# Expert outputs of a decoder trunk on one Trainium2 core: rows scattered to token order from GpSimd's queue, or whole slot blocks stored from ScalarE's queue and gathered by token at the end

## The chip, the cores and the metric

One Trainium2 chip, one core. The time is device microseconds of one launch, from run to run; the kernel before took 1139.21 us (median of 3 runs, 1138.52 to 1142.39).

## What is computed

A decoder layer on 512 tokens of width 1024 in float32: a mixed attention and recurrent stage, a cross-attention into 256 memory tokens, and a mixture of experts, each followed by a layer norm of `ALPHA*x + result`. Only the last stage is touched. Its reference, cut:

```
e_idx, gate = route(xf, w_router, b_router)      # best of 8 groups, then top-2 of its 4 experts
# for each expert e, over the rows (tokens) that chose it:
h = jax.nn.silu(xb @ w_gate[e]) * (xb @ w_up[e])
y = h @ w_down[e]
# back to tokens, each row weighted by its gate, the two rows of a token added:
y = segment_sum(y * row_gate[:, None], row_tok)
x = layer_norm(ALPHA * x + y, ln_g[l, 2], ln_b[l, 2])
```

There are 32 experts, each with gate and up weights of 1024 x 512 and down weights of 512 x 1024: 6 MB for an expert, 192 MB in all. The 512 tokens choose 2 experts each, so 1024 rows exist, 32 for an expert on average.

## The kernel before, in words

All times and lines here are of the last stage, from about 605 us on.

**Slots.** Each expert gets a block of `CAP` = 64 slots. A table `tabs` (128 x 32 x 4) holds for each slot of each expert the token, the destination row and the two factors (gate, and ALPHA for the first choice of a token). It is made by matmuls of one-hot masks (`token_columns`, L1425; `row_and_gate_columns`, L1432) that DVE reads out of PSUM (L1439, L1443 to L1447). Empty slots get indices beyond the bounds. A token that overflows 64 slots is handled by `further_blocks`, a loop that runs only if some expert has more than 64 rows; in the profiled execution it does not run.

**Weights.** SP alone issues the weights, in pieces of 1 MB (128 partitions x 8 KB), in the order of use (`stream`, `load_piece`, L1482) into 21 places. For piece n it waits until its place is free and until piece n-4 has landed (`piece_here(sp, n - 4)`, L1485), so about four pieces are outstanding.

**One expert.** POOL gathers its token rows with an indirect DMA from DRAM (`xs_rows`) into 64 partitions of `xg` (`rows_in`, L1771). PE turns them (L2003, L2004), ACT copies the result (`tokens`, L2229), PE multiplies gate and up (`gate_up`, L2020), ACT takes the silu (L2234), DVE the product (L2450), PE turns that, DVE copies (L2454), PE multiplies down (`down`, L2030), and DVE scales by the gate and adds ALPHA times the token rows that ACT has prepared (`first_rows`, L2241) into `ye` (`out_rows`, L2464). `ye` is 128 x 512: partitions 0 to 63 hold the first half of the 64 result rows, 64 to 127 the second. It has two buffers.

**Results out.** After each expert POOL waits for DVE and scatters `ye` with an indirect DMA into `y_rows`, a DRAM table in token order (row = choice, token, half; 2 KB each), L1776. Empty slots are skipped. In POOL's program the gather for expert e+2 stands ahead of the scatter of expert e. The last two experts (30 and 31) are different: only their ALPHA part (`xrow`) is scattered, their products are brought into token order by PE (`combined`, L2125).

**The tail.** SP waits for all scatters (`rows_out`, `late_out`), then loads `y_rows` back in four transfers of 1 MB, one for each 128 tokens (`yb[t]`, L1708), with the gain and offset of the layer norm between the second and the third (L1707). DVE or PE add the two rows of each token (L2506, L2118), the layer norm follows (DVE L2513 to L2530, ACT L2299), and SP stores the output (L1711).

## Time and profile before

| what | value |
|---|---|
| median of 3 runs | 1139.21 us (1138.52 to 1142.39) |
| span of the profiled execution | 1135.4 us |
| its own time as a run | not recorded apart; the median is 3.8 us above the span |
| PE busy | 1058.4 us, 93% |
| DVE / ACT / POOL busy | 345.5 / 273.6 / 85.8 us |
| the core's DMA, whole span | 263.31 MB, 232 GB/s |
| HBM read / written | 257.60 / 13.05 MB |

The span runs from the first to the last instruction; a run's time has some microseconds of launch around it. MB are millions of bytes, while a weight piece is 1024 KB. "DMA share" is the mean busy share of the core's 16 DMA engines; it can pass 1 a little where transfers of an engine overlap. "PEclk" is TensorE's granted clock as a share of 2.4 GHz. SPq, ACTq and POOLq are the queues' issuing side. The number in square brackets behind a row of the timeline is the time for which the engine stood idle before it, and who ended that.

### The profile page before, as it was taken

Reading aid. Unit: us, or ns where it says so; the run is one execution under the profiler, and the core shown is the slowest. Engines: PE = TensorE matmul, PEld = TensorE weight load, DVE = VectorE, ACT = ScalarE, POOL = GpSimd, SP = SyncE. Lnnn points to the kernel's source line nnn. Section 1 sums busy time; section 2 is a strip of 40 time slices with the busy share of each in tenths; the row PEclk is TensorE's granted clock in tenths of the full one; section 3 lists DMA queues with packets and bytes.
Section 4 is the critical chain, followed back from the end, with each engine's and each line's share of the span. In section 5 each row is a group of like instructions: output and inputs, shape, how many; then the busy total and the mean of one; then the engine's idle time right before and its main releaser. Section 6 shows DMA issues by size and latency. Waiting matters only on the chain.

```text
span 1135.4 us, 15981 instructions
## 1 busy us (share of the span) xinstructions
PE 1058.4 (93%) x6710; PEld 533.3 (47%) x6710; DVE 345.5 (30%) x729; ACT 273.6 (24%) x540; POOL 85.8 (8%) x133
## 2 busy tenths in 40 slices
PE   9999999999899999999998999999998898898896
PEld 4444455566655544566446544444443333333332
DVE  0179522334664453104146211111111011011116
ACT  2431122234454500023202211222111011011123
POOL 2000100000000000100000211111111101101110
PEclk9999999999999999999999899999999989989999
DMA  8112220222024320923316999999999999999996
GB/s 278 37 41 86 97 76 2 76 76 76 14 64 149 110 77 1 361 84 117 148 74 257 368 398 404 403 394 393 393 396 392 401 395 394 399 396 401 398 401 251
DMA packets 55847, 263.31 MB, mean 232 GB/s; under 512 B 7250, under 2 KB 8402, under 8 KB 30944
## 3 DMA queue, kind: packets, MB, share of 16 engines
q1 hardware_dynamic: 49424, 252.81, 57.8%
q0 software_dynamic: 5120, 8.40, 2.3%
q8 instruction: 54, 0.88, 0.3%
q10 hardware_dynamic: 1232, 1.07, 0.3%
q14 instruction: 17, 0.14, 0.0%
HBM read 257.60 MB, written 13.05 MB: 238 GB/s over the span
## 4 chain that ended last, share of the span: by engine, by line
PE 31%; DMA 24%; DVE 3%; issue 1%; ACT 1%; SPq 0%; POOLq 0%; ACTq 0%; DVEq 0%
DMA ring<-in_w_exp_up 7%; PE cpair L2020 5%; PE bank L2030 5%; PE tpair L2020 4%; DMA ar<-in_w_exp_up 3%; PE bank L1861 2%; PE bank L1841 2%; DMA mixT<-in_w_exp_down 2%; DMA ring<-in_w_exp_down 2%; DMA avq<-in_w_exp_up 2%; PE tpair L1861 1%; PE bank L1834 1%; PE cpair L1861 1%; PE tpair L1841 1%; PE cpair L1841 1%; DMA mixT<-y_rows 1%
## 5 line engine op out<-in xcount | busy, mean ns | idle before, releaser
L2020 PE MATMUL cpair<-ring,xgT 128*64 128x512 f32 x312 | 82.8, 594 | 7.6 <-DMA ring<-in_w_exp_up 4.4
L2234 ACT ACTIVATE hs<-cpair 64x512 f32<-64x512 f32 x21 | 12.4, 589 | 237.7 <-PE cpair L2020 237.7
L2464 DVE SCALAR_TENSOR_TENSOR ye<-bank,tabs,xgt 128x512 f32<-128x512 f32 x30 | 22.5, 751 | 136.0 <-PE bank L2030 136.0
L2030 PE MATMUL bank<-ring,hT 128*64 128x512 f32 x224 | 57.6, 656 | 6.2 <-DVE hT L2454 6.2
L2450 DVE TENSOR_TENSOR hs<-cpair,hs 64x512 f32<-64x512 f32 x21 | 14.6, 693 | 154.3 <-ACT hs L2234 154.3
L922 PE MATMUL bank<-xT,ring 128*128 128x512 f32 x128 | 60.9, 606 | 0.0
L1776 POOL DMA_INDIRECT y_rows<-ye,tabs x30 | 30.3, 1011 | 383.8 <-DVE ye L2464 383.8
L2020 PEld LDWEIGHTS cpair<-ring,xgT 128*64 128x64 f32 x312 | 26.2, 137 | 53.1 <-issue 52.0
L365 PE MATMUL bank<-xT,ring 128*128 128x512 f32 x112 | 48.5, 593 | 0.0
L2241 ACT ACTIVATE xgt<-xgt,tabs 64x512 f32<-64x512 f32 x64 | 46.0, 719 | 1.6
L2020 PE MATMUL tpair<-ring,xgT 128*64 128x512 f32 x152 | 39.5, 594 | 4.5 <-DMA ring<-in_w_exp_up 2.5
L941 PE MATMUL tpair<-ring,mixT 128*128 128x512 f32 x96 | 42.0, 593 | 0.0
L1012 ACT ACTIVATE pcb<-tpair 128x512 f32<-128x512 f32 (+1 forms) x32 | 17.4, 544 | 77.3 <-DVE pcb L1180 77.2
L2450 DVE TENSOR_TENSOR hs<-tpair,hs 64x512 f32<-64x512 f32 x11 | 7.6, 693 | 90.7 <-ACT hs L2234 90.7
L2030 PEld LDWEIGHTS bank<-ring,hT 128*64 128x64 f32 x224 | 16.5, 151 | 37.6 <-issue 29.8
L365 PEld LDWEIGHTS bank<-xT,ring 128*128 128x128 f32 x112 | 21.2, 190 | 27.1 <-issue 26.3
L2229 ACT ACTIVATE xgT<-tpair 128x512 f32<-128x512 f32 x32 | 19.1, 597 | 58.4 <-PE tpair L2004 58.4
L2004 PEld LDWEIGHTS tpair<-ident,xgt 64*128 64x128 f32 x224 | 32.5, 223 | 0.0
L2234 ACT ACTIVATE hs<-tpair 64x512 f32<-64x512 f32 x11 | 6.5, 588 | 107.6 <-PE tpair L2020 107.6
L922 PEld LDWEIGHTS bank<-xT,ring 128*128 128x128 f32 x128 | 22.3, 190 | 20.7 <-issue 19.8
L1771 POOL DMA_INDIRECT xgt<-xs_rows,tabs x31 | 29.6, 955 | 15.7 <-issue 9.0
L911 PE MATMUL bank<-memT,ring 128*128 128x256 f32 x128 | 30.7, 383 | 0.0
(471 smaller groups left out, 1894.7 us busy)
## 6 DMA issues: line engine op xcount, KB each, us to landing
ring<-in_w_exp_gate SPq DMA_DIRECT2D x30, 1024.0 KB, 11.1
ring<-in_w_exp_down SPq DMA_DIRECT2D x30, 1024.0 KB, 11.1
ring<-in_w_exp_up SPq DMA_DIRECT2D x28, 1024.0 KB, 11.2
ring<-in_w_in SPq DMA_DIRECT2D x6, 2048.0 KB, 8.1
ring<-in_w_mem_kv SPq DMA_DIRECT2D x4, 2048.0 KB, 10.3
mixT<-in_w_exp_down SPq DMA_DIRECT2D x7, 1024.0 KB, 10.3
ar<-in_w_exp_down SPq DMA_DIRECT2D x7, 1024.0 KB, 11.0
xT<-in_w_exp_gate SPq DMA_DIRECT2D x6, 1024.0 KB, 11.5
```

The costliest lines, as they stand in the source:

```text
L365: last = nc.tensor.matmul(dst[:, :], w[:, k, j * P:(j + 1) * P], xT[:, k, :], start=(k == 0), stop=(k == KT - 1))
L911: last = nc.tensor.matmul(dst[:, a * MEM:(a + 1) * MEM], slot(GKV + i // 2, 512)[:, k, ct * P:(ct + 1) * P], memT[:, k, :], start=(k == 0) ...
L922: last = nc.tensor.matmul(dst[:, :], lhs, rhs, start=(k == 0), stop=(k == KT - 1))
L941: last = nc.tensor.matmul(wo_bank[i % 3][:, :], mixT[:, k, t * P:(t + 1) * P], slot(GO + hf, 512)[:, k, :], start=(k == 0), stop=(k == 2 * ...
L1771: return pool.indirect_dma_start(dst, None, xs_rows[:, :], bass.IndirectOffsetOnAxis(idx.bitcast(U32), 0), bounds_check=below(S), oob_is_e ...
L1776: return pool.indirect_dma_start(y_rows[:, :], bass.IndirectOffsetOnAxis(idx.bitcast(U32), 0), src, None, bounds_check=below(TOP_K * S * 2 ...
L1841: last = nc.tensor.matmul(bank[NT * hf + t][:, :], omT[:, k, t * P:(t + 1) * P], w[:, k, :], start=(k == 0), stop=(k == KT - 1))
L1861: last = nc.tensor.matmul(bank[i][:, cs], w[:, k, (i % 4) * P:(i % 4 + 1) * P], x1T[:, k, cs], start=(k == 0), stop=(k == KT - 1))
L2004: return nc.tensor.transpose(dst, src, ident[rows, rows])
L2020: last = nc.tensor.matmul(bank[b][m * CAP:(m + 1) * CAP, :], xgT[:, k, :], w(m, h)[:, j * DE:(j + 1) * DE], start=(k == 0), stop=(k == KT ...
L2030: last = nc.tensor.matmul(bank[b][m * CAP:(m + 1) * CAP, :], ht[:, k, :], w(2, h)[:, o:o + 512], start=(k == 0), stop=(k == FT - 1))
L2241: nc.scalar.activation(xrow[half[h], e % 2, :], xg[half[e % 2], h * 512:(h + 1) * 512], ACT.Copy, scale=tabs[half[e % 2], e, 3:4].bitcast( ...
```

## The change

The table in token order is gone. A new DRAM table `y_first` has one row of 4 KB for every slot of every expert (32 x 64 rows), and `y_further` has the slots of further blocks. Four things happen.

- **Stores.** ACT issues, for each of experts 0 to 29, two plain DMAs (`result_out`): partitions 0 to 63 of `ye` to the first half, and 64 to 127 to the second half of 64 consecutive rows. All 64 slots are stored, filled or not. In ACT's program `result_out(e - 1)` stands ahead of `silu(e)`, and waits for DVE's `y_scaled`. `token_rows_out` does the same for experts 30 and 31. POOL's scatters are gone from the loop, only its gathers are left.
- **Collecting.** When all stores have landed, POOL issues eight indirect gathers of 128 rows x 4 KB from `y_first` into `yb[t]`, two for each t, in place of SP's four loads. SP loads only the layer norm's gain and offset, right behind the weights.
- **Routing.** DVE computes where the two rows of each token lie (`slot_at`): six small operations more, and the two that made the destination rows and the ALPHA factors are gone. The table columns for destinations are gone.
- **The path for overflow** clears `y_further` first and collects from it afterwards; it does not run on this input.

```
-            KEPT = 905
+            KEPT = 904
 
             def __init__(self, flat):
                 self.kept = flat[:, 0:self.KEPT]
                 self.sel_rows = flat[:, 0:768].rearrange("p (k t f e) -> p k t f e", k=TOP_K, t=NT, f=3)
-                self.caps, self.place, self.row_off = flat[:, 768:896], flat[:, 896:904], flat[:, 904:905]
+                self.caps, self.place = flat[:, 768:896], flat[:, 896:904]
                 self.hit = flat[:, 1024:2048].rearrange("p (r c) -> p r c", c=2 * CAP)
+                self.erow = flat[:, 1024:1024 + NE]
...
-        tabs = sb("tabs", [P, NE, 4], I32)
+        toks = sb("toks", [P, NE], I32)
+        gates = sb("gates", [P, 2, NE])
...
-        def tokens_read(dve, n):
+        def tokens_read(dve, to, n):
             dve.wait_ge(tab_full, 2 * n - 1)
-            nc.vector.tensor_scalar(tabs[0:CAP, :, 0], bank[6][0:CAP, 0:NE], float(OFF), None, ALU.add).then_inc(tokens_known, 1)
-
-        def rows_and_gates_read(dve, ls, n):
+            nc.vector.tensor_scalar(to[0:CAP, :], bank[6][0:CAP, 0:NE], float(OFF), None, ALU.add).then_inc(tokens_known, 1)
+
+        def gates_read(dve, to, n):
             dve.wait_ge(tab_full, 2 * n)
-            nc.vector.tensor_scalar(tabs[:, :, 1], bank[7][:, 0:NE], ls.row_off[:, 0:1], None, ALU.add)
-
-            nc.vector.tensor_scalar(tabs[:, :, 3].bitcast(F32), bank[7][:, 0:NE], 2.0 * S - 2.0 * OFF, ALPHA, ALU.is_lt,
-                                    ALU.mult)
-            nc.vector.tensor_copy(tabs[:, :, 2].bitcast(F32), bank[7][:, NE:2 * NE]).then_inc(tabs_done, 1)
+            nc.vector.tensor_copy(to[:, :, :].rearrange("p f e -> p (f e)"), bank[7][:, 0:2 * NE]).then_inc(tabs_done, 1)
...
-        y_rows = nc.dram_tensor("y_rows", (TOP_K * S * 2, D // 2), F32, kind="Internal").ap()
+        SLOTS, FURTHER = NE * CAP, (S // CAP - 1) * NE * CAP
+        y_first = nc.dram_tensor("y_first", (SLOTS, D), F32, kind="Internal").ap()
+        y_further = nc.dram_tensor("y_further", (FURTHER, D), F32, kind="Internal").ap()
+        y_half_rows = y_further.rearrange("r (h c) -> (r h) c", h=2)
...
-                    rows_out(sp)
-                    sp.wait_ge(late_out, 32)
                     down_read(sp, LAST - 2)
                     sp.wait_ge(f_end, more * NE + 1)
-                    for t in range(NT):
-                        if t == 2:
-                            for h, src in enumerate((ln_g, ln_b)):
-                                sp.dma_start(ln3[:, h, :], src[0, 2:3, :].to_broadcast([P, D])).then_inc(n3.here, 16)
-                        sp.dma_start(yb[t], y_v[t * P:(t + 1) * P, :, :]).then_inc(y_read[t], 16)
+                    for h, src in enumerate((ln_g, ln_b)):
+                        sp.dma_start(ln3[:, h, :], src[0, 2:3, :].to_broadcast([P, D])).then_inc(n3.here, 16)
                     for t in range(NT):
                         sp.wait_ge(n3.shifted, t + 1)
                         sp.dma_start(out[0, t * P:(t + 1) * P, :], ob[t]).then_inc(out_done, 16)
...
+                    def collect(dst, src, rows, idx):
+                        return pool.indirect_dma_start(dst, None, src,
+                                                       bass.IndirectOffsetOnAxis(idx.bitcast(U32), 0),
+                                                       bounds_check=below(rows), oob_is_err=False)
...
                         rows_in(e + 2)
-                        pool.wait_ge(y_scaled, e + 1)
-                        scatter(tabs[:, e, 1:2], ye[:, e % 2, :]).then_inc(y_out[e % 2], 16)
...
-                    further_blocks(pool, before, body)
-                    for e in PE_LAST:
-                        pool.wait_ge(x_done, 2 * (e + 1))
-                        scatter(tabs[:, e, 1:2], xrow[:, e % 2, :]).then_inc(late_out, 16)
+                    def after():
+                        for t in range(NT):
+                            for k in range(TOP_K):
+                                r = k * NT + t
+                                collect(yb[t][:, k, :], y_further[:, :], FURTHER, further_at[:, r:r + 1])\
+                                    .then_inc(f_back, 16)
+                        pool.wait_ge(f_back, 16 * TOP_K * NT)
+
+                    further_blocks(pool, before, body, after)
+                    rows_out(pool)
+                    pool.wait_ge(late_out, 64)
+                    down_read(pool, LAST - 2)
+                    for t in range(NT):
+                        for k in range(TOP_K):
+                            r = k * NT + t
+                            collect(yb[t][:, k, :], y_first[:, :], SLOTS, slot_at[:, r:r + 1]).then_inc(y_read[t], 16)
...
                         if t == 2:
-                            pe.wait_ge(y_read[t], 16)
+                            pe.wait_ge(y_read[t], 32)
...
+                    def result_out(e):
+
+                        act.wait_ge(y_scaled, e + 1)
+                        for h in range(2):
+                            act.dma_start(y_first[e * CAP:(e + 1) * CAP, h * 512:(h + 1) * 512], ye[half[h], e % 2, :])\
+                                .then_inc(y_out[e % 2], 16)
+
+                    def token_rows_out(e):
+
+                        act.wait_ge(x_done, 2 * (e + 1))
+                        for h in range(2):
+                            act.dma_start(y_first[e * CAP:(e + 1) * CAP, h * 512:(h + 1) * 512], xrow[half[h], e % 2, :])\
+                                .then_inc(late_out, 16)
...
                     for e in range(LAST - 1):
+                        if e:
+                            result_out(e - 1)
                         silu(e)
...
                             tokens(e + 1)
                             first_rows(e + 1)
+                    result_out(LAST - 2)
...
                     tokens(e)
                     first_rows(e)
+                    token_rows_out(e)
                     gu_read(act, e)
                     tokens(f)
                     first_rows(f)
+                    token_rows_out(f)
...
+                    link(dve, V.tensor_tensor(ohr[:, :, :, :], oh[:, 0:TOP_K, :, :],
+                                              ls.erow[:, :].unsqueeze(1).unsqueeze(1).to_broadcast(wide), ALU.mult))
+                    link(dve, V.tensor_reduce(slot_f[:, :], ohr[:, :, :, :].rearrange("p k t e -> p (k t) e"), AX_X,
+                                              ALU.add))
...
+                    rows = TOP_K * NT
+                    link(dve, V.tensor_tensor(past[:, :, :], ls.thresholds[:, :].unsqueeze(1).to_broadcast([P, rows, S // CAP - 1]),
+                                              ls.place[:, :].unsqueeze(2).to_broadcast([P, rows, S // CAP - 1]), ALU.is_le))
+                    link(dve, V.tensor_tensor(slot_f[:, :], slot_f[:, :], ls.place[:, :], ALU.add))
+                    tokens_read(dve, toks, 1)
+                    link(dve, V.tensor_reduce(blk_of[:, :], past[:, :, :], AX_X, ALU.add))
+                    link(dve, V.scalar_tensor_tensor(slot_at[:, :], blk_of[:, :], float(NE * CAP - CAP), slot_f[:, :], ALU.mult,
+                                                     ALU.add))
...
-                            dve.wait_ge(y_out[e % 2], 16 * (e // 2))
+                            dve.wait_ge(y_out[e % 2], 32 * (e // 2))
```

ACT's queue in the loop over the experts, before: from the silu of one expert to that of the next (`xgt` holds the gathered rows and, in its second half, their scaled copy; `ye` is the result).

```order
L2234 ACTIVATE hs<-cpair 64x512 [waits w_read]
L2229 ACTIVATE xgT<-tpair 128x512 [waits xgt_full]
L2241 ACTIVATE xgt<-xgt,tabs 64x512 [waits y_scaled]
L2241 ACTIVATE xgt<-xgt,tabs 64x512
L2234 ACTIVATE hs<-cpair 64x512 [waits w_read]
L1612 TENSOR_LOAD more_i
```

The same place in the change.

```order
L2267 ACTIVATE hs<-cpair 64x512 [waits w_read]
L2262 ACTIVATE xgT<-tpair 128x512 [waits xgt_full]
L2274 ACTIVATE xgt<-xgt,gates 64x512 [waits y_scaled]
L2274 ACTIVATE xgt<-xgt,gates 64x512
L2281 DMA y_first<-ye 64x512 [waits y_scaled]
L2281 DMA y_first<-ye 64x512
L2267 ACTIVATE hs<-cpair 64x512 [waits w_read]
L2281 DMA y_first<-ye 64x512 [waits y_scaled]
L2281 DMA y_first<-ye 64x512
```

Two DMA issues, the first of them behind a wait for DVE's result, have come in between the scaled rows and the next silu.

POOL's queue at the end of the loop and behind it, before (the overflow branch between them is left out).

```order
L1767 REGISTER_ALU [waits x_done,xgt_full]
L1771 DMA xgt<-xs_rows,tabs 64x1024
L1767 REGISTER_ALU [waits y_scaled]
L1776 DMA y_rows<-ye,tabs 2048x512
L1612 TENSOR_LOAD more_i
...
L1767 REGISTER_ALU [waits x_done]
L1776 DMA y_rows<-xgt,tabs 2048x512
L1767 REGISTER_ALU [waits x_done]
L1776 DMA y_rows<-xgt,tabs 2048x512
L1622 UNCONDITIONAL_BRANCH
```

POOL in the change.

```order
L1775 REGISTER_ALU [waits x_done,xgt_full]
L1779 DMA xgt<-xs_rows,toks 64x1024
L1775 REGISTER_ALU [waits x_done,xgt_full]
L1779 DMA xgt<-xs_rows,toks 64x1024
L1618 TENSOR_LOAD more_i
...
L1775 REGISTER_ALU [waits late_out,w_read,y_out1,y_out0]
L1788 DMA xT<-y_first,blkones 128x1024
L1775 REGISTER_ALU
L1788 DMA xT<-y_first,blkones 128x1024
...
L1775 REGISTER_ALU
L1788 DMA mixT<-y_first,blkones 128x1024
L1630 UNCONDITIONAL_BRANCH
```

The scatters are gone, and eight gathers from `y_first` stand at the end, behind the wait that SP had.

SP's queue behind the last weights, before.

```order
L1703 ISA [waits late_out,w_read,y_out1,y_out0]
L1708 DMA xT<-y_rows 128x2x1024 [waits f_end]
L1708 DMA xT<-y_rows 128x2x1024
L1707 DMA avq<-in_ln_g 128x1024
L1707 DMA avq<-in_ln_b 128x1024
L1708 DMA mixT<-y_rows 128x2x1024 x2
L1711 DMA out<-ring 128x1024 [waits ln2_shifted] x4
L1622 UNCONDITIONAL_BRANCH [waits out_done]
```

SP in the change.

```order
L1714 ISA [waits w_read]
L1716 DMA avq<-in_ln_g 128x1024 [waits f_end]
L1716 DMA avq<-in_ln_b 128x1024
L1719 DMA out<-ring 128x1024 [waits ln2_shifted] x4
L1630 UNCONDITIONAL_BRANCH [waits out_done]
```

The four loads of `y_rows` have left SP, and the gain and offset no longer wait for the scatters.

## Rows read from the trace of the kernel before

**Rows 1.** Stages: window, its length, busy us of each engine, PEclk, DMA share, GB/s

```profile
700.00:800.00 100.00, 96.09 (x462) 40.61 (x460) 13.83 (x22) 18.37 (x28) 14.76 (x15) 1.00 1.02 400
1000.00:1085.00 85.00, 72.48 (x312) 29.49 (x309) 9.72 (x16) 11.08 (x17) 9.82 (x10) 0.93 1.01 402
```

**Rows 2.** Chain that ended last, from 770 us: start us, us, what

```profile
770.17 6.87 PE cpair L2020 x32
783.64 6.87 PE cpair L2020 x32
...
803.81 11.19 DMA ar<-in_w_exp_up
...
1062.53 9.87 DMA ar<-in_w_exp_up
```

**Rows 3.** Waits of SP's queue, 600 to 1136 us: total us, times, longest

```profile
SPq L1485 <- DMA ring<-in_w_exp_down: 63.2, 24, 3.7
```

**Rows 4.** Page, section 3: DMA queues, packets, MB, share of 16 engines

```profile
q1 hardware_dynamic: 49424, 252.81, 57.8%
q0 software_dynamic: 5120, 8.40, 2.3%
```

**Rows 5.** Windows around one scatter and one gather (columns as in 1)

```profile
867.00:870.00 3.00, 2.99 (x14) 1.24 (x16) 0.00 (x0) 0.00 (x0) 1.96 (x2) 1.00 1.02 412
871.50:873.00 1.50, 1.01 (x6) 0.53 (x8) 0.00 (x0) 0.00 (x0) 0.00 (x0) 1.00 1.01 418
873.00:876.00 3.00, 3.00 (x16) 1.16 (x13) 0.00 (x0) 0.33 (x1) 0.00 (x0) 1.00 1.06 303
```

**Rows 6.** Timeline of POOL, the issues of these two, and a gather alone

```profile
635.58 0.93 POOL L1771 DMA_INDIRECT xgt<-xs_rows,tabs  x1 [6.69 <-ACT xgt L2241]
...
867.60 1.01 POOL L1776 DMA_INDIRECT y_rows<-ye,tabs  x1 [11.20 <-DVE ye L2464]
868.91 0.95 POOL L1771 DMA_INDIRECT xgt<-xs_rows,tabs  x1 [0.30 <-issue]
```

**Rows 7.** Windows with a gather alone, and with scatters alone

```profile
635.00:640.00 5.00, 5.00 (x26) 1.58 (x22) 0.00 (x0) 1.06 (x1) 0.93 (x1) 1.00 0.99 328
1090.00:1095.00 5.00, 5.00 (x27) 2.31 (x23) 0.00 (x0) 0.00 (x0) 0.00 (x0) 1.00 1.01 414
```

**Rows 8.** Timeline, the way into the last experts and their scatter

```profile
1084.62 0.75 DVE L2464 SCALAR_TENSOR_TENSOR ye<-bank,tabs,xgt 128x512 f32<-128x512 f32 x1 [5.55 <-PE bank L2030]
1085.95 0.60 ACT L2229 ACTIVATE xgT<-tpair 128x512 f32<-128x512 f32 x1 [9.14 <-PE tpair L2004]
1091.58 8.22 SPq L1482 DMA_DIRECT2D ring<-in_w_exp_down  x4
1097.15 0.57 ACT L2234 ACTIVATE hs<-tpair 64x512 f32<-64x512 f32 x1
1098.02 0.99 POOL L1776 DMA_INDIRECT y_rows<-xgt,tabs  x1 [8.16 <-ACT xgt L2241]
```

**Rows 9.** Timeline, the tail: loads of y_rows and who waited

```profile
1104.64 1.77 SPq L1708 DMA_DIRECT2D xT<-y_rows  x2
1107.46 1.16 SPq L1708 DMA_DIRECT2D mixT<-y_rows  x2
1112.40 1.22 DVE L2506 TENSOR_TENSOR xT<-xT 128x1024 f32<-128x1024 f32 x1 [3.56 <-DMA xT<-y_rows]
1120.60 1.98 PE L2118 MATMUL cpair<-mixT,ident 128*128 128x512 f32 x4 [0.99 <-DMA mixT<-y_rows]
```

**Rows 10.** Timeline, routing

```profile
620.32 0.42 DVE L2403 TENSOR_TENSOR pmT<-oh,bank 128x256 f32<-128x256 f32 x1 [0.84 <-PE bank L1987]
```

**Rows 11.** Window in the tail (columns as in 1)

```profile
1115.00:1120.00 5.00, 4.61 (x22) 1.74 (x18) 4.45 (x8) 1.54 (x3) 0.00 (x0) 1.00 1.00 409
```

**Rows 12.** DMA issues: median us to landing, 1085 to 1136 us

```profile
y_rows<-xgt,tabs POOLq DMA_INDIRECT x2, 6.9
```

**Rows 13.** The same for the gathers, whole span

```profile
DMA to landing us min/median/max: 7.2/8.1/8.6
```

103 lines of the change are left out of this document (68 added, 35 removed).

## The prediction, made before the changed kernel was run

> **What bounds the kernel now.** I read first the table of stages. In the expert stage the 16 DMA engines are busy for 1.01 to 1.02 of each window and move 400 and 402 GB/s, while PE falls from 96% busy to 85% [rows 1]. Then the chain of waits: up to 803 us it runs through PE, and from there to 1072 us it is, but for two short pieces, one weight transfer after the other [rows 2]. Then what the loader waits for: SP stands not at a full place but at its own piece four back (63.2 us for one group of 24; two dozen more groups read alike) [rows 3]. So the stage is bound by bytes through the engines. PE needs 13.47 us for an expert where nothing holds it (from one gate-and-up product to the next, 770.17 to 783.64) [rows 2], the 6.29 MB of an expert need 15.7 us at 400 GB/s. Whatever adds bytes between 640 and 1110 us moves everything behind it; whatever saves POOL or DVE time there is worth nothing.
>
> **What the change adds.** The software queue (POOL's) moved 8.40 MB in the whole span [rows 4]. The 1024 filled rows of 4 KB are 4.19 MB, and they are gathered once and scattered once: 8.39 MB. So empty slots move no bytes today. The change stores all 32 x 64 slots of 4 KB, 8.39 MB where 4.19 MB were scattered: 4.19 MB more, in rows of 2 KB as before.
>
> Price of a MB: the weight queue took 57.8% of 1135.4 us for 252.81 MB, 2.60 us per MB of all 16 engines; the software queue 2.3% for 8.40 MB, 3.11 us [rows 4]. Do writes ride along free, beside reads? One scatter was issued at 867.60 us and one gather at 868.91 [rows 6]; with a landing some 7 to 8 us behind the issue [rows 12, 13], their bytes fall at about 871.5 to 876. While the first, the scatter's, are moved the total is 418 GB/s, against 412 before them [rows 5]: it does not rise by what is written. So a written byte displaces a read one, and I take 4.19 x 2.60 = **+10.9 us**. Lower end: all stores at the weight queue's price, the scatters given back at the software queue's, 21.8 - 13.0 = +8.8. Upper end: the stores at 3.11, the scatters given back at 2.60, 26.1 - 10.9 = +15.2. I take the value between because the windows with scatters show neither gain nor loss beyond the bytes [rows 5, 7].
>
> The Trainium skill (DMA: Bandwidth & Descriptors, Specifications) gives a fabric ceiling of 435 GB/s; by it the added bytes would cost 9.6 us, an estimate from that page. The same table puts the limit of HBM for a core at about 358 GB/s; the trace stands above that, at 400 to 414 GB/s [rows 1, 7], so the measurement decides.
>
> **What it moves.**
> - *POOL.* It loses 32 scatters of 1.0 us and the long waits for DVE. Nobody waited for POOL, so +0. The gather for expert e+2 no longer stands behind the scatter of the expert before and comes some 5 us earlier; its data had time already.
> - *ACT in the loop.* Two issues per expert, 0.6 to 0.9 us each by SP's rows (1.16 and 1.77 us for two) [rows 9], behind a wait for DVE's result. That result is ready just after the down product, and the silu is due a whole gate-and-up product (6.87 us of PE) later [rows 2]. Hidden, +0. What queues behind the wait is the silu; it would show only if a store were not issued in time.
> - *DVE* waits until the store of the expert two before has landed, some 27 us after its issue. Hidden.
> - *The end of the loop.* Here the cover is thin. DVE's last result ends at 1084.62 + 0.75 = 1085.37 and ACT's next copy, on PE's path, began at 1085.95 [rows 8]. Two issues between them end at 1086.5 to 1087.1: 0.6 to 1.2 us on a PE chain that has no wait for weights behind it. The same again ahead of the silu at 1097.15 [rows 8], where PE first has half a product of expert 31 to do: hidden.
> - *The tail.* ACT's last scaled rows end at 1097.2. The scatter issued at 1098.02 had landed by 1104.6, when SP went on [rows 8, 9], some 6.9 us after its issue [rows 12]. The new store is plain and as small; I give it the same time, so POOL starts its gathers at about 1104.5 (all tail times before the shift). Eight at 1.0 + 0.3 us [rows 6]: the sixth, which completes t = 2, is issued at 1111.1 and lands with the gathers' 8.1 us [rows 13] by 1119.2; the eighth by 1121.8. The bytes, 4.19 MB plus 1.05 MB of gain and offset, take 12.8 us at 409 GB/s [rows 11], to 1117.4. Before, the same block reached PE at 1120.60, and PE had then been idle for only 0.99 us [rows 9]. So at most 1.0 us is gained there, however much earlier the rows come. DVE stood idle for 3.56 us for the first block [rows 9], but it then needs PE's sums. Tail: -1.0 to +1.2, I take 0.
> - *Routing.* Two of the new DVE operations (0.42 us each, as L2403) stand where DVE was idle for 0.84 us [rows 10]; of four smaller ones, the two reads of the table that fall away make up a part. At most two such operations' 0.8 us on PE's start, in a stretch where PE is still ahead of the weights' end: +0.
>
> Sum: 1135.4 + 10.9 = 1146.3 us of span. The median of the runs is 3.8 us above the span, so **1150.1 us**.
>
> **The rivals.**
> 1. *The dip goes with the scatter (faster).* Right after each pair of scatter and gather the rate falls to 303 GB/s for some 3 us [rows 5], that is (412 - 303) x 3 = 327 KB or 0.79 us; over 30 experts 24 us. Taken from the stage's 401 GB/s against 412, it is 11/412 x 440 us = 12 us. If two software transfers back to back cause it, the change takes it away: +10.9 - 18 = -7, **1132 us**. It decides if more than half of the dips go. Against it: a gather alone, issued at 635.58 [rows 6], has its window at 328 GB/s, and two scatters without a gather keep theirs at 414 [rows 7]. The dip belongs to the gather, which stays. Chance 0.10.
> 2. *Stores from half the partitions dip too.* What sets the gather apart is that it touches 64 partitions, and each new store touches 64 as well. One more such dip for each expert is 12 to 24 us: 1150 + 18 = **1168 us**; a dip for each of both stores would give 1186. Against it: the gather writes into SBUF, as the weights do, and a store reads from it. No 64-partition store stands in the trace. Chance 0.13. The Trainium skill (DMA: Bandwidth & Descriptors, The descriptor swizzle) says that in a transfer to 128 partitions each engine writes a port of its own; by it a transfer on 64 would put two engines on one port. The dips of the gathers agree; for stores no run shows it yet.
> 3. *The last gathers are slow.* If reading scattered rows, not the half partitions, makes the dip, the 4.19 MB at the end move at 303 instead of 409 GB/s: 13.8 instead of 10.3 us, +3.6, **1154 us**. Against it, nothing but the partitions. Chance 0.10.
> 4. *The stores are free.* They go the idle way, and the time stays at **1139 us**. The scatter's window (418, not more) speaks against it [rows 5]. Chance 0.05.
>
> **How the numbers follow.** The forecast has 0.62. A measurement of this kernel can tell 0.3% (3.4 us) from no change. Faster is rival 1, 0.10; within 0.3% is rival 4, 0.05; slower is the forecast with rivals 2 and 3, 0.85. The forecast by itself spans 1147 (+8.8 and -1.0) to 1156 (+15.2 and +1.2). The range runs from 1146, a little below that, to 1170, which takes in rival 3 and the one-dip case of rival 2; left out are rivals 1 and 4 and the worse half of 2.
>
> **What the profile after would show.** HBM written up by 4.2 MB; ACT's queue with 8.4 MB; POOL's at 8.4 MB still. Between 700 and 1085 us the DMA share stays at 1.01 to 1.02 and the total rate near 400 GB/s; the last weights are issued 10 to 11 us later than 1099.8. Down to 350 GB/s would be rival 2; up to 412 rival 1; above 420 rival 4. The last gather lands within 18 us of the last store for the forecast. Wrong altogether would be a stage in which the DMA share falls below 1: then a wait (DVE for a store, or the silu for its turn) has taken over.

## The result, and the profile after

The changed kernel takes 1145.87 us (median of 17 runs, 1142.64 to 1149.25), the kernel before 1140.33 us beside it (17 runs): a ratio of 1.0046, 95% interval 1.0035 to 1.0057, or about +5 us. The forecast was 1150.1 us, range 1146 to 1170. Slower was right, the size was half of what was said, and the time lies just outside the range. Told as a difference the miss is plainer: +10.9 us was forecast, +8.8 us at the lowest for the bytes, and +5.2 us by the ratio (4.0 to 6.5) was measured. The profiled execution of after ran for 1145.51 us with a span of 1143.5, an offset of 2.0 us.

Its windows (columns as in [rows 1]):

```profile
700.00:800.00 100.00, 96.07 (x456) 40.54 (x454) 13.83 (x22) 18.37 (x28) 7.50 (x8) 0.98 1.02 405
1000.00:1085.00 85.00, 73.74 (x315) 29.67 (x317) 9.34 (x15) 11.60 (x18) 4.68 (x5) 0.92 1.02 408
1090.00:1095.00 5.00, 4.80 (x16) 1.51 (x18) 0.00 (x0) 1.59 (x3) 0.00 (x0) 0.66 1.02 418
1110.00:1115.00 5.00, 4.48 (x23) 1.88 (x21) 1.12 (x2) 2.40 (x4) 2.56 (x3) 1.00 0.59 201
1115.00:1120.00 5.00, 5.00 (x26) 1.76 (x24) 1.17 (x1) 0.60 (x1) 3.78 (x5) 1.00 0.88 283
```

The stage is still bound by DMA (share 1.02) and moves 405 and 408 GB/s where it moved 400 and 402 [rows 1]. In the tail, between 1110 and 1120 us, the engines are not full for 10 us; before they moved 409 GB/s from 1115 to 1120 [rows 11].

The DMA queues of after (as in [rows 4]):

```profile
q1 hardware_dynamic: 48336, 248.61, 55.9%
q0 software_dynamic: 3712, 8.40, 2.3%
q10 hardware_dynamic: 6352, 9.47, 2.2%
HBM read 257.60 MB, written 13.05 MB: 237 GB/s over the span
```

ACT's queue (q10) has its 8.4 MB more, and POOL's its 8.40 MB, as forecast. HBM written stands at 13.05 MB in both kernels.

The stage is measured from POOL's first gather to the issue of the last weights. The first gather of the kernel before:

```profile
624.45 1.33 POOL L1754 DMA_INDIRECT xgt<-xs_rows,tabs  x1 [3.63 <-DVE tabs L1439]
```

The timeline of after, from the first gather to the tail:

```profile
624.45 1.21 POOL L1762 DMA_INDIRECT xgt<-xs_rows,toks  x1 [3.74 <-DVE toks L1441]
...
1085.90 0.75 DVE L2528 SCALAR_TENSOR_TENSOR ye<-bank,gates,xgt 128x512 f32<-128x512 f32 x1 [3.85 <-PE bank L2063]
1086.68 1.51 ACTq L2281 DMA_DIRECT2D y_first<-ye  x2
1089.55 0.60 ACT L2262 ACTIVATE xgT<-tpair 128x512 f32<-128x512 f32 x1 [9.77 <-issue]
1090.20 5.35 PE L2053 MATMUL tpair<-keys,xgT 128*64 128x512 f32 x16 [3.08 <-ACT xgT L2262]
1093.34 8.53 SPq L1480 DMA_DIRECT2D ring<-in_w_exp_down  x4
1102.56 1.10 ACTq L2288 DMA_DIRECT2D y_first<-xgt  x2
1111.83 1.03 POOL L1788 DMA_INDIRECT xT<-y_first,blkones  x1 [42.44 <-PE bank L2063]
1118.83 1.23 DVE L2581 TENSOR_TENSOR xT<-xT 128x1024 f32<-128x1024 f32 x1 [4.31 <-DMA xT<-y_first,blkones]
1122.31 1.23 DVE L2581 TENSOR_TENSOR xT<-xT 128x1024 f32<-128x1024 f32 x1 [2.25 <-DMA xT<-y_first,blkones]
1131.69 2.08 PE L2151 MATMUL bank<-mixT,ident 128*128 128x512 f32 x2 [2.76 <-DVE mixT L2581]
```

The last of the four weight issues began at 1093.34 + 8.53 - 0.33 = 1101.54, 477.1 us behind the first gather; before at 1091.58 + 8.22 - 0.33 = 1099.47 [rows 8], 475.0 us behind it. So the stage grew by 2.1 us, not by 10 to 11. From there to the end it took 42.0 us, against 35.9; of these two parts the end is the larger one in this pair of profiles. At the end of the loop PE stood 3.08 us idle, waiting for a copy of ACT. The chain of waits says what ACT did between its two stores and that copy:

```profile
1088.22 0.72 ACTq L1618
...
1090.20 8.78 PE tpair L2053 x32
...
1103.05 7.87 DMA y_first<-xgt
```

L1618 is the register read of the overflow branch; it now stands behind ACT's wait for the last result. The product behind the gap took 8.78 us, with a mean granted clock of 0.66 in 1090 to 1095: part of it ran at 1.2 GHz and part at 2.4, after PE had stood idle for 3.08 us. The last stores were then issued 4.5 us later than the last scatter was [rows 8], of which 2.1 us are the stage. From there to the first read of the table it took 9.3 us (1102.56 to 1111.83), against 6.6 before (1098.02 to 1104.64) [rows 8, 9], and from there to the end 31.7 us against 30.8. Together these are the 8.1 us by which the two spans differ.

### The profile page after: what moved, and what is told of

It is laid out like the page before. It is cut to its first block, busy times and chain, and to the rows that moved or that the text cites. A ratio compares the mean times of both kernels' runs of the same rounds, so it can differ in the third digit from the quotient of the medians.

```text
span 1143.5 us, 15997 instructions
## 1 busy us (share of the span) xinstructions
PE 1059.1 (93%) x6710; PEld 532.3 (47%) x6710; DVE 346.8 (30%) x733; ACT 273.8 (24%) x540; POOL 61.0 (5%) x109
## 3 DMA queue, kind: packets, MB, share of 16 engines
HBM read 257.60 MB, written 13.05 MB: 237 GB/s over the span
## 4 chain that ended last, share of the span: by engine, by line
PE 35%; DMA 19%; DVE 4%; issue 1%; ACT 1%; ACTq 0%; POOLq 0%; POOL 0%; SPq 0%; DVEq 0%
PE cpair L2053 7%; PE bank L2063 6%; PE tpair L2053 5%; DMA ring<-in_w_exp_up 5%; DMA ring<-in_w_exp_down 3%; PE bank L1894 2%; PE bank L1874 2%; DMA ar<-in_w_exp_down 2%; DMA xT<-in_w_exp_up 2%; DMA keys<-in_w_exp_up 2%; DMA mixT<-in_w_exp_up 2%; PE tpair L1894 1%; PE bank L1867 1%; PE cpair L1894 1%; PE tpair L1874 1%
## 5 line engine op out<-in xcount | busy, mean ns | idle before, releaser
L2528 DVE SCALAR_TENSOR_TENSOR ye<-bank,gates,xgt 128x512 f32<-128x512 f32 x30 | 22.5, 751 | 133.4 <-PE bank L2063 133.4
L2063 PE MATMUL bank<-ring,hT 128*64 128x512 f32 x224 | 55.1, 632 | 6.2 <-DVE hT L2518 6.2
L1779 POOL DMA_INDIRECT xgt<-xs_rows,toks x31 | 29.1, 938 | 412.3 <-ACT xgt L2274 412.2
L2274 ACT ACTIVATE xgt<-xgt,gates 64x512 f32<-64x512 f32 x64 | 46.0, 719 | 1.6
L922 PE MATMUL bank<-ring,memT 128*128 128x512 f32 x64 | 30.5, 599 | 0.0
## 6 DMA issues: line engine op xcount, KB each, us to landing
ring<-in_w_exp_gate SPq DMA_DIRECT2D x30, 1024.0 KB, 10.8
```

What stands on the lines that cost most here:

```text
L922: last = nc.tensor.matmul(dst[:, :], lhs, rhs, start=(k == 0), stop=(k == KT - 1))
L1779: return pool.indirect_dma_start(dst, None, xs_rows[:, :], bass.IndirectOffsetOnAxis(idx.bitcast(U32), 0), bounds_check=below(S), oob_is_e ...
L2063: last = nc.tensor.matmul(bank[b][m * CAP:(m + 1) * CAP, :], ht[:, k, :], w(2, h)[:, o:o + 512], start=(k == 0), stop=(k == FT - 1))
L2274: nc.scalar.activation(xrow[half[h], e % 2, :], xg[half[e % 2], h * 512:(h + 1) * 512], ACT.Copy, scale=gates[half[e % 2], 1, e:e + 1]).th ...
L2528: V.scalar_tensor_tensor(ye[:, e % 2, :], bank[5][:, :], gates[:, 0, e:e + 1], xrow[:, e % 2, :], ALU.mult, ALU.add).then_inc(y_scaled, 1)
```

## The experiments

Times are medians, ratios are to the kernel before on the same chip. A difference in us between kernels of different groups is the difference of their ratios times 1140 us. "Stage" is the last weights' issue less the first gather's issue, "end" the rest of the span, both of one profile. "Beside" is the mean rate in a window of 8 us that begins 3 us behind each gather's issue, over the 24 to 26 gathers between 690 and 1060 us.

A stage comes from one profile each. Four kernels whose loop is the same (changed, its last stores from POOL, and the two with plain loads at the end) have stages of 476.7 to 478.2 us, so a stage can be told to 1 to 2 us. There is only one profile of the kernel before, and that execution was some 3 us faster than its median, so a difference to its 475.0 may be off by as much. An interval of a ratio is 1 to 3 us wide to either side.

| kernel | median us (runs) | ratio, 95% interval | stage, end us | beside, GB/s |
|---|---|---|---|---|
| before | 1140.33 (17) | 1 | 475.0, 35.9 | 385 |
| changed | 1145.87 (17) | 1.0046 (1.0035 to 1.0057) | 477.1, 42.0 | 388 |
| before, no scatters | 1124.35 (6) | 0.9878 (0.9851 to 0.9905) | 461.4, 35.6 | 386 |
| changed, no stores | 1126.13 (6) | 0.9895 (0.9872 to 0.9918) | 459.8, 37.6 | 386 |
| before, gather parted | 1138.05 (12) | 0.9987 (0.9974 to 1.0000) | 472.2, 35.8 | 385 |
| changed, gather beside | 1140.03 (12) | 0.9996 (0.9979 to 1.0013) | 470.9, 39.0 | 399 |
| changed, gather after | 1146.80 (8) | 1.0050 (1.0032 to 1.0068) | 479.5, 38.8 | 382 |
| changed, POOL's stores | 1144.30 (8) | 1.0041 (1.0024 to 1.0058) | 477.4, 38.3 | 390 |
| changed, stores twice | 1164.24 (5) | 1.0217 (1.0192 to 1.0241) | 498.5, 38.2 | 384 |
| before, wide gather | 1130.26 (6) | 0.9915 (0.9892 to 0.9937) | 458.0, 42.2 | 418 |
| changed, wide gather | 1135.15 (10) | 0.9950 (0.9935 to 0.9965) | 463.6, 37.6 | 416 |
| wide, no scatters | 1129.90 (4) | 0.9904 (0.9888 to 0.9920) | 447.3, 56.0 | |
| before, empty scatters | 1129.68 (6) | 0.9906 (0.9881 to 0.9931) | 463.5, 35.9 | 380 |

### What the stores and the scatters cost

Both kernels without their results out; the waits for them go too, and the last gathers or loads read weights. The changed kernel, then the kernel before:

```
-                        if e:
-                            result_out(e - 1)
...
-                    result_out(LAST - 2)
```

```
-                        pool.wait_ge(y_scaled, e + 1)
-                        scatter(tabs[:, e, 1:2], ye[:, e % 2, :]).then_inc(y_out[e % 2], 16)
```

> The changed kernel without the stores of experts 0 to 29 and the waits for them; the gathers at the end read rows of the expert weights in place of the slot table, so the results of those experts are left out. Theory 2 (bytes): 7.86 MB at 2.6 us per MB of the DMA-bound stage are 20 us, and the stall goes too: 1120 to 1124. Rival (a byte stored costs less than a byte loaded): 1130 to 1136. The gathers' dips stay in either.

> The kernel before without the scatters of experts 0 to 29 and the waits for them; the loads at the end read weights in place of the row table, so the results of those experts are left out. Theory 3 (a scatter costs its bytes and a part of the dip behind it): 3.93 MB cost 10 us and the dips another 6 to 8, so 1122 to 1124, the same as the changed kernel without stores. Rival (a scatter costs its bytes alone): 1130.

The stores cost 1.0046 - 0.9895 = 1.51%, or 17.2 us (14.3 to 20.1), for 7.86 MB: 2.2 us per MB. The scatters cost 1.22%, or 13.9 us (10.8 to 17.0), for 3.93 MB: 3.5 us per MB. The profiles say the same of the stage alone, 17.3 and 13.6 us. The forecast had taken 2.60 for both. The difference of the two costs, 3.3 us, is itself uncertain by 4.2 us. The time without stores lies between the theory's and the rival's; the time without scatters is 0.35 us above the theory's range, and the rival, bytes alone, falls.

Are plain stores of 64 partitions at their bytes' price when there are more of them? Each result stored a second time:

```
+                            act.dma_start(y_copy[e * CAP:(e + 1) * CAP, h * 512:(h + 1) * 512], ye[half[h], e % 2, :])\
+                                .then_inc(y_out[e % 2], 16)
```

> The changed kernel, in which ACT stores each result of experts 0 to 29 twice, the second time into a table that nobody reads: 7.86 MB of plain stores more, and two issues more for each expert on ACT. Taking the stores away gave back 19.7 us, 2.5 us per MB. Theory that plain stores cost their bytes and no more: +18 to +21 us, 1164 to 1167 us, ratio 1.021 to 1.024, the last weights issued 18 to 20 us later than in the changed kernel. Rival, the measured 19.7 us holds a fixed part that is paid once (the waits at the end of the loop and the tail): +14 us or less. Rival, four issues for each expert hold up ACT's silu: more than +25 us, and windows of the stage in which the DMA share falls below 1.

+1.71%, 19.5 us (16.4 to 22.5) for 7.86 MB, 2.5 us per MB, and 21.4 us of the stage, as expected. Beside the gathers the rate is 384 GB/s, near the 388 of single stores. Stores cost their bytes and no dip of 12 us or more comes with them: rival 2 of the prediction falls.

### Where the gather stands

In the kernel before, the gather moved ahead of the wait for the scatter:

```
+                    rows_in(2)
                     for e in range(LAST - 1):
-                        rows_in(e + 2)
+                        if e + 3 < NE:
+                            rows_in(e + 3)
                         pool.wait_ge(y_scaled, e + 1)
```

> The kernel before, with each gather put ahead of the wait for the scatter on POOL's queue, so that gather and scatter lie some 5 us apart. Theory 3a (the dip is worse where scatter and gather follow each other): 4 to 8 us faster, 1132 to 1136. Theory 3b (each costs what it costs alone): within 1.5 us of 1140.3.

1.5 us less by the ratio (its interval just reaches 1), 2.8 us less of the stage. The 4 to 8 us of the first theory did not come, and the time alone can't tell the 1.5 us from nothing. In the changed kernel the gather was then put back to where it had been, first beside the stores, then behind them:

```
                     for e in range(LAST - 1):
+                        if e:
+                            pool.wait_ge(y_scaled, e)
                         rows_in(e + 2)
```

> The changed kernel, in which POOL issues the gather for expert e+2 only once DVE has finished the result of expert e-1, as it did before the change, so that the gather runs beside ACT's two stores and not about 5 us ahead of them. Parting gather and scatter in the kernel before gave back 1.9 us. Theory that a small write beside the gather costs more than its bytes, whichever queue it comes from: 1148 to 1149 us, ratio 1.007 to 1.008. Rival, only two transfers of the software queue get in each other's way: no difference to the changed kernel, 1145 to 1146 us, ratio 1.004 to 1.006, stage windows 400 to 405 GB/s.

1140.03 us, 5.7 us less than the changed kernel (within 2.3 either way), where I had expected 2 to 3 us more; the rival, no difference, missed too. The theory was wrong in sign. The stage is 6.2 us shorter. Timeline of this run, ACT's queue and POOL:

```profile
869.37 1.10 ACTq L2283 DMA_DIRECT2D y_first<-ye  x2
...
870.10 0.93 POOL L1779 DMA_INDIRECT xgt<-xs_rows,toks  x1 [12.53 <-DVE ye L2530]
```

and its windows behind them:

```profile
873.00:875.00 2.00, 1.75 (x9) 0.76 (x11) 0.00 (x0) 0.00 (x0) 0.00 (x0) 1.00 1.02 416
875.00:877.00 2.00, 2.00 (x11) 0.68 (x7) 0.00 (x0) 0.06 (x1) 0.00 (x0) 1.00 1.04 348
```

In the changed kernel the same gather was issued 4.9 us ahead of the stores (866.81 against 871.71; over the 24 gathers it is 3.2 us for 14 of them and 4.6 to 4.9 for the rest), and its dip is nearly the old one, 321 GB/s where [rows 5] have 303:

```profile
870.00:871.00 1.00, 1.00 (x6) 0.28 (x4) 0.07 (x1) 0.00 (x0) 0.00 (x0) 1.00 1.02 426
871.00:874.00 3.00, 3.00 (x16) 0.84 (x12) 0.68 (x1) 0.00 (x0) 0.00 (x0) 1.00 1.03 321
```

The new theory: while a gather is moved, something is free that a store can use. It was tested by moving the gather further, behind the stores:

```
+                            pool.wait_ge(y_out[(e - 1) % 2], 32 * ((e + 1) // 2))
```

> The changed kernel, in which POOL issues the gather for expert e+2 only when both stores of expert e-1 have landed, about 10 us after it stood in the run beside the stores and about as much after its place in the changed kernel. The gather beside the stores gave 1140.0 us, the gather ahead of them 1145.9. Theory that the stores fill the room that the half-partition gather leaves, when both are moved at once: here it is lost again, 1144 to 1148 us, ratio 1.004 to 1.007, stage windows near 402 GB/s. Rival, it only matters that the gather is issued late, not that the stores are under way: 1138 to 1142 us, windows near 408 GB/s.

1146.80 us: the gain is gone again. The timeline shows the gather released by a landed store (the stores in question were issued at 856.88):

```profile
865.80 0.93 POOL L1779 DMA_INDIRECT xgt<-xs_rows,toks  x1 [12.91 <-DMA y_first<-ye]
```

The gathers of this run stand between two pairs of stores, 14 of 24 nearer to the pair that comes next (3.6 to 7.8 us later). What matters is whether the bytes move at the same time, and the packets in the traces show it. Counted from the issue of a gather, its own packets fall at 4 to 6 us in all three kernels. Those of the stores fall at 8 to 11 us in the changed kernel, at 3 to 7 us in the run beside the stores, and in this one those of the next pair come at 9 us and later.

Beside the gathers the mean rate is 399 GB/s with stores under way, 388 with the gather ahead of them and 382 behind them. So the change lost 5.7 us by letting the gather run ahead, an edit that the forecast had put at nothing.

Then the plain stores were put into the scatter's place, in POOL's program and queue:

```
                         rows_in(e + 2)
+                        pool.wait_ge(y_scaled, e + 1)
+                        for h in range(2):
+                            pool.dma_start(y_first[e * CAP:(e + 1) * CAP, h * 512:(h + 1) * 512], ye[half[h], e % 2, :])\
+                                .then_inc(y_out[e % 2], 16)
```

> The changed kernel, in which POOL and not ACT issues the two plain stores of each expert 0 to 29, at the place in its program where the scatter stood: the same bytes as the changed kernel, in the queue and next to the gather as before the change. Theory that the queue and the place made the difference, not the form: a gather on POOL's queue stands behind the stores, so they cannot fill its room, and the whole 4.19 MB at 2.5 to 2.6 us are paid against the scatters: 1149 to 1152 us, ratio 1.008 to 1.011. Rival, the indirect form was dear and plain stores are cheap wherever they stand: 1144 to 1147 us, as the changed kernel.

1144.30 us, no difference to the changed kernel that can be told (-0.6 us, within 2.3 either way): the rival was right. The stores (16.26 MB in POOL's queue) stand 1.5 us ahead of the gather:

```profile
871.22 1.06 POOL L1806 DMA_DIRECT2D y_first<-ye  x2 [15.57 <-DVE ye L2529]
872.76 0.99 POOL L1779 DMA_INDIRECT xgt<-xs_rows,toks  x1 [0.48 <-issue]
```

Close in time, but out of the same queue, they gain nothing by the gather (390 GB/s beside it), nor do they lose. So the neighbour in the queue alone did not make the scatter dear. That it is the queue which keeps these stores from gaining is argued from this one run, in which the stores are also issued somewhat further ahead of the gather (1.5 us, where it was 0.7 from ACT).

### The gather on all partitions

Token rows as 128 half rows of 2 KB into 128 partitions; PE turns 16 pieces of 64x64, ACT makes one scaled copy. The core of it, in the kernel before:

```
-                        gather(xg[half[e % 2], :], tabs[0:CAP, e, 0:1]).then_inc(xg_here[e % 2], 16)
+                        gather(xg[:, e % 2, :], tabs[:, e, 0:1]).then_inc(xg_here[e % 2], 16)
```

> The kernel before, in which an expert's token rows are gathered as 128 half rows of 2 KB into all 128 partitions, instead of 64 rows of 4 KB into 64 partitions; the same bytes. PE turns them by 16 products of 64x64 instead of 8 of 64x128, ACT makes one scaled copy of 128x512 instead of two of 64x512. Theory that the fall of the rate to about 303 GB/s beside each gather comes from its use of only half the partitions: the fall goes, 0.4 to 0.8 us for each expert, 1116 to 1128 us, ratio 0.980 to 0.990, 3 us behind a gather's start the rate stays near 400. Rival, the fall comes from scattered reads or from the software queue's small packets: 1138 to 1144 us, ratio 0.998 to 1.003, the fall still there or wider.

and with the gather parted from the scatter, as above:

> The wide gather of the run before this one, and the gather for expert e+3 issued ahead of POOL's wait for the result of expert e, so that gather and scatter lie some 5 us apart. If adjacency of the two software transfers costs by itself: 2 us less than the wide gather alone. If the wide gather removes what adjacency cost, no difference to it. If this beats both kernels it is the version to keep: 1114 to 1128 us where the theory of the half partitions holds, 1137 to 1139 where it does not.

1130.26 and 1128.97 us (the second: 0.9916, 0.9888 to 0.9945), 10 us below the kernel before. Both times stand 1 to 2 us above what the theory gave, but the fall is gone, which is what it stood on, and the rival's 1138 us and more did not come. Parting gather and scatter gives nothing more here (stage 459.3 against 458.0). The windows of the first:

```profile
863.00:866.00 3.00, 3.00 (x38) 2.01 (x34) 0.69 (x1) 0.59 (x1) 0.00 (x0) 1.00 1.04 427
...
700.00:800.00 100.00, 96.39 (x597) 44.10 (x595) 13.02 (x22) 12.56 (x21) 14.30 (x14) 0.98 1.01 417
1000.00:1085.00 85.00, 80.22 (x457) 34.67 (x455) 10.09 (x16) 8.97 (x15) 12.23 (x12) 0.93 1.01 417
```

The gather was issued at 860.36, and where the rate had fallen to 303 it is 427. The stage is 17.0 us shorter, and 6 of them are given back at the end (42.2 against 35.9). PE is now the tighter one: from 1000 to 1085 us it is busy for 80.22 us, where it was 72.48 [rows 1], and ACT's last scaled rows end 4.2 us behind the issue of the last weights, where they had ended 2.2 us ahead of it. The Trainium skill (DMA: Bandwidth & Descriptors, The descriptor swizzle) gives each engine a port of its own where a transfer has 128 partitions. The trace agrees as far as it goes, with 385 GB/s beside the half gather and 418 beside the wide one; no run here shows the ports.

The edit also makes the rows 2 KB instead of 4 KB, and no run changes the one without the other. Against the row length as the cause speak the eight gathers at the end of the changed kernel, with rows of 4 KB into all 128 partitions. Their packets keep the 16 engines busy for 2.8 us per MB (4.19 MB, 59.6% of 1111 to 1131 us), though with hardly any weights beside them. In the stage the wide gather has 2.65 (3.99 MB, 2.4% of 640 to 1080 us, in the run without scatters below), the half gather 3.45 (3.95 MB, 3.1% of the same window, in the kernel before without scatters).

The same edit on the changed kernel, then with the gather beside the stores, by the wait shown above:

> The changed kernel with the wide gather: 128 half rows of 2 KB into 128 partitions, as it was tried on the kernel before (1130.3 us). Its last weights were issued 458.0 us behind the first gather there. Theory that the change adds 4.19 MB and that there is no dip left for the scatters to have widened: the last weights 10 us later, at 468 us behind the first gather, the end +4 to +10 us against the wide gather without the change, since PE is near its own bound there (48 of 50 us busy): 1134 to 1140 us, ratio to the kernel before 0.995 to 1.000. Rival, scatters cost more than their bytes even beside a wide gather: +2 us or less, 1130 to 1132 us.

> The changed kernel with the wide gather, issued beside the stores. Theory that the stores gained only by filling the room beside a half-partition gather: with the wide gather the place of the gather is worth nothing, the same time as in the run before this one within 1.5 us. Rival, reads and writes under way together gain by themselves: 4 to 6 us less than in the run before this one, as with the narrow gather.

1135.15 us: +0.35% or 4 us (within 3 either way) against the wide gather alone. That is in the range that was expected, but of the stage it is 5.6 us, where 10 had been expected. Beside the stores 1132.22 us (0.9941, 0.9921 to 0.9961), 1.0 us less by the ratios and 2.9 by the medians, which can't be told from nothing. The stage decides, 463.8 against 463.6: the place of the gather is worth nothing there where there is no dip to fill, while it was worth 6.2 us with the narrow gather. None of the pair beats the wide gather without the change.

### What a scatter costs by itself

The wide gather and the kernel before without its scatters, the two edits shown above together:

> The kernel before with the wide gather and without the scatters of experts 0 to 29 (their results reach no output; the loads at the end read weights). The wide gather with its scatters had its last weights issued 458.0 us behind the first gather and took 1130.3 us; with the narrow gather the scatters cost 13.6 us of the stage, 3.4 to 4.0 us per MB. Theory that a scatter costs its bytes and the rest is its meeting with the narrow gather: the last weights 9 to 10.5 us earlier, at 447.5 to 449 us, if PE lets them. Rival, a scatter has a price of its own: 13 us or more. Since PE is busy for 48 of 50 us, PE can hide it: the run then ends at 1124 to 1129 us.

With the wide gather the stage is 10.7 us shorter without scatters, against 13.6 with the narrow one. The 2.9 us between them are the size of the 2.8 us that parting the two had given back. Both figures rest on the one profile of the kernel before. The run itself stays at 1129.9 us, as with the scatters: PE hides all of it.

The last run keeps the scatters and takes their bytes away, by a bound that skips nearly every row:

```
-                    def scatter(idx, src):
+                    def scatter(idx, src, rows=TOP_K * S * 2):
...
-                                                       src, None, bounds_check=below(TOP_K * S * 2), oob_is_err=False)
+                                                       src, None, bounds_check=below(rows), oob_is_err=False)
...
-                        scatter(tabs[:, e, 1:2], ye[:, e % 2, :]).then_inc(y_out[e % 2], 16)
+                        scatter(tabs[:, e, 1:2], ye[:, e % 2, :], 1).then_inc(y_out[e % 2], 16)
```

> The kernel before, in which the scatters of experts 0 to 29 are issued as ever but with a bound that lets every row but the first of the table fall away: they carry no results (the end reads weights in their place). Without the scatters altogether it took 0.9878 of the kernel before, some 13.9 us less. Theory that a scatter has a price of its own beside the bytes of its filled rows, in its skipped rows and its place beside the gather: 2 to 5 us of the 13.9 stay, ratio 0.990 to 0.992. Rival, a scatter costs only what its filled rows carry, at 3.5 us per MB: as without scatters, 0.987 to 0.989. The page counts 7.87 MB less written to HBM where the scatters are gone, though the queues moved 3.94 MB less: if skipped rows are written somewhere, this run shows it in that row.

2.1 us of stage stay (463.5 against 461.4), 3.2 us by the ratio (within 4 either way). Queue and HBM rows of this run:

```profile
q0 software_dynamic: 5120, 4.47, 1.5%
...
HBM read 257.60 MB, written 13.05 MB: 240 GB/s over the span
```

and of the kernel without scatters:

```profile
q0 software_dynamic: 2720, 4.46, 1.3%
...
HBM read 257.60 MB, written 5.18 MB: 234 GB/s over the span
```

2400 packets more with 0.01 MB in them take 0.2% of the engines' span, some 2 us. So a scatter is not free when all its rows are skipped, as I had taken it to be: it moves no bytes, but it has packets. There are as many of them (5120 in the queue) as in the kernel before, where the rows are filled [rows 4]. Of the 2.1 us only a part can therefore be laid to skipped rows in the kernel before: there 1024 of 2048 rows are skipped, here nearly all, and what of it is owed to a row and what to a scatter no run tells. The time lies in the theory's range, though by its interval it can't exclude the rival.

### The end of the loop and the tail

The two stores of the last looped expert issued from POOL, where they stand in nobody's way:

```
+                        pool.wait_ge(y_scaled, LAST - 1)
+                        for h in range(2):
+                            pool.dma_start(y_first[(LAST - 2) * CAP:(LAST - 1) * CAP, h * 512:(h + 1) * 512],
+                                       ye[half[h], (LAST - 2) % 2, :]).then_inc(y_last, 16)
...
-                    result_out(LAST - 2)
```

> The changed kernel, with the two stores of expert 29 alone issued from POOL's queue instead of ACT's. Theory 1 (the stall at the end of the loop): in the changed kernel ACT waits for the result of expert 29, issues two stores, and only then loads the register for the overflow branch; PE stands idle 3.08 us for ACT's copy and its next product runs 8.8 us instead of 7.1 at the lower clock. Without that: 4 to 5 us less than the changed kernel, about 1141. Rival (the added bytes set the end, PE's stall is covered): within 1 us of 1145.9.

PE's gap shrank to 0.75 us, the median is 1145.84 us (1.0059, 1.0037 to 1.0081): no gain, where the theory had 4 to 5 us; the rival was right. In this profile a later product ran at a clock of 0.66 (1100 to 1105 us) and the end took 38.9 us. Next, with the gather beside the stores, the register read ahead of the wait:

```
+                    early = act.value_load(more_i[0:1, 0:1], min_val=0, max_val=S // CAP - 1)
                     result_out(LAST - 2)
```

> The gather beside the stores (1140.0 us), and ACT reads the register of the overflow branch ahead of its wait for expert 29's result, not behind it. Theory that the 0.7 us of the register read lie on the way to the last two experts: 1138.5 to 1139.5 us. Rival, that way has slack, or the two stores alone hold it up: 1140.0 us, no difference that can be told. It would be 1137 or less if the whole stall of 3.1 us in the changed kernel were owed to it.

1139.50 us (12 runs; 0.9991, 0.9974 to 1.0007), 0.5 us below the run without it, within their intervals, so theory and rival can't be told apart. PE's gap is 1.66 us, where it was 2.70:

```profile
1087.56 3.65 PE L2055 MATMUL tpair<-keys,xgT 128*64 128x512 f32 x16 [1.66 <-ACT xgT L2264]
```

So the read costs 1.0 us of gap, but none of it is seen in the end of this profile (40.4 us, where it was 39.0). Last, four plain loads from SP in place of the eight gathers (tokens then get rows that are not theirs):

```
-                            collect(yb[t][:, k, :], y_first[:, :], SLOTS, slot_at[:, r:r + 1]).then_inc(y_read[t], 16)
+                        sp.dma_start(yb[t], y_v[t * P:(t + 1) * P, :, :]).then_inc(y_read[t], 16)
```

> The changed kernel, in which four plain loads of 1 MB from SP read the table's first 1024 rows at the end, in place of the eight gathers (the rows of a token are therefore not its own: the collecting by token is left out). Without stores and scatters the end took 2.0 us longer with gathers than with loads, in one profile each. Theory that the gathers' issues on POOL and their landing cost 2 to 3 us: 1143 to 1144 us. Rival, what is lost at the end is the wait for the last stores, not the gathers: 1145 to 1147 us.

1149.86 us (1.0078, 1.0063 to 1.0092), slower, because I had also put the load of the norm's gain and offset behind the four:

```profile
1129.62 1.28 DVE L2596 SCALAR_TENSOR_TENSOR ring<-xT,blkones,avq 128x1024 f32<-128x1024 f32 x1 [3.00 <-DMA avq<-in_ln_b]
```

With that load put back ahead of the wait:

> As in the run with plain loads at the end (the rows of a token are not its own there either), but the gain and offset of the layer norm are loaded ahead of the wait for the stores, as in the changed kernel; behind the four loads they had held DVE up for 3.0 us. Theory that the eight gathers' issues and landing cost 2 to 3 us more than four plain loads: 1143 to 1144 us. Rival, the end is set by the wait for the last stores, and the gathers are as good as loads: 1145 to 1147 us.

1144.83 us (5 runs; 1.0055, 1.0042 to 1.0069), stage 478.2, end 38.6: no difference to the changed kernel with its gathers that can be told (+0.09% or 1 us, within 2). The theory's 2 to 3 us less did not come. The eight gathers are as good as four loads.

## Why the prediction was wrong in size

**The bound.** Right: DMA share 1.02, rate near 400, PE waiting for weights. All that took bytes away or gave the engines a better rate shortened the stage.

**Bytes.** Right in MB (+4.2 in the queues, rows of 2 KB), wrong in one row: the page's HBM written does not rise, since it counts the slots a scatter is issued for, skipped ones too (13.05 MB with empty scatters).

**The step that failed** is "so a written byte displaces a read one, and I take 4.19 x 2.60 = +10.9 us": one price for what comes and what goes. The stores cost 17.2 us where 7.86 x 2.60 = 20.4 was taken. The weight queue's 2.60 [rows 4] has the gathers' dips in it; away from the gathers the changed kernel moves 421 GB/s (mean of 24 windows from 3 us ahead of a gather's issue to 2 us behind it), which is 2.37 us per MB. The scatters gave back 13.9 us where 10.2 was taken: the bytes (3.93 x 2.37 = 9.3), 1 to 2 us for what an empty scatter costs, and some 3 us for their meeting with the half-partition gather; the last two are estimates from single profiles. 17.2 - 13.9 = +3.3 us, within 4.2. The other 1.9 us of the 5.2 stand between the two kernels when neither has its results out (0.9895 and 0.9878, ends of 37.6 and 35.6 us). Even the lower end, +8.8, had the stores at 2.60; with 2.37 and the software queue's own 3.11 [rows 4] it would have been 19.9 - 13.0 = +6.9. The scatter's window of 418 against 412 GB/s [rows 5] could not price a transfer whose cost lies in what it does to its neighbour.

**POOL, +0.** This step failed too, and the sum hides it. "Its data had time already" is true, but the gather's place decides what it overlaps: beside the stores 5.7 us less. With its place kept, the change would have cost nothing that can be told (0.9996). So the forecast stood as near as it did because two errors went against each other: the bytes were taken too dear, and the gather's new place was taken to be free.

**ACT's loop, DVE's waits.** Right: twice the stores on ACT cost their bytes and left the share at 1.02.

**The end of the loop, 0.6 to 1.2 us.** The place was right, the size not: 3.08 us of gap, with the register read behind the stores (0.72 us and its issue), which the order of ACT's program showed, and a lower clock in the product behind it. In the medians it is hardly seen: taking it away gave nothing that can be told.

**The tail, 0.** Gathers against loads: right. But the end of the span took 42.0 us in the changed kernel and 38 to 39 us in most variants with stores and the narrow gather (38.2 to 39.0 in six, 40.4 in one, and 43.7 where the gain was loaded late), against 35.9 before and 37.6 without stores. A part of it is "I give it the same time": from the end of ACT's last scaled rows to the first read of the table it took 9.3 us (1102.5 to 1111.83) where the forecast had 7.3 (1097.2 to 1104.5) and the kernel before 7.4. In the other kernels with stores and the narrow gather it is 7.8 to 9.0 us, but 9.0 in the kernel before with its gather parted, so this is no clean price of a store. The rest was not settled; moving the stores off ACT and taking the gathers away both left the end at 38 us and more. That the last gather would land within 18 us of the last store's landing came true: it was issued at 1121.23 and landed at most 6.5 us later (the eight took 4.5 to 6.5 us), with the store landed at about 1110.9, so 16.8 us at most.

**The rivals.** The dip does belong to the gather, as said against rival 1: taking the scatters away left 386 GB/s beside it. Rival 3 falls too, since scattered reads into all partitions made no dip. Rival 4 had a grain in it: stores are partly free, but only beside a gather on half the partitions.

**The offset.** In all the other profiled executions a run is 1.5 to 2.1 us longer than its span. By that the profiled execution of before took some 1137.4 us, and about half of the 3.8 us, 1.8, was its own good luck against the median of three. It was carried along rightly, since before and forecast stand on the same level. That level was itself 1.1 us below the median of 17 runs (1140.33), so the forecast came 1.1 us nearer to the measured time than its +10.9 us deserved.

## What to carry to other kernels

In this DMA-bound stage a byte had no single price: price what is removed from a run without it, not from its queue's mean, and look at what each transfer overlaps. A gather into half the partitions lowered the rate of everything for 3 us here; making it full width won 10 us, more than the whole change cost, and where that can't be done, a store from another queue issued at the same moment fills part of the hole. Before trading scatters with skipped rows for dense stores, count both the padding and the packets that a scatter has even for skipped rows.

## What the runs showed of the hardware

- The same bytes gathered to 128 instead of 64 partitions: 418 instead of 385 GB/s in the 8 us beside a gather, 17.0 us of stage over 30 experts. The rows were halved to 2 KB by the same edit.
- Plain stores beside the half gather: 399 GB/s, ahead of or behind it 382 to 388, and out of the gather's own queue 390, with no gain in time. The DMA share stands at 1.03 to 1.06 in the dips shown, so the share alone does not show it. That a gather leaves free what a store uses is argued from these rates; which part of the chip it is, no run told.
- Scatters whose rows are nearly all skipped carry no bytes but cost: 30 of them had 2400 packets with 0.01 MB, some 2 us of 16 engines (1.5% against 1.3% of the span), and 2.1 us of stage. The page's HBM written counts their slots all the same (13.05 against 5.18 MB).
- 4 KB rows gathered from a table at the end, 4.19 MB in eight transfers, took as long as four plain loads of 1 MB, as far as can be told (1.0046 against 1.0055).
